# Page numbers read four at a time, and the experts' sub-keys moved to other slots, in a two-layer decoder step

## What is computed

```python
mla_past = cache_mla[i][page_table].reshape(B, past_len, KV_LORA + D_ROPE)
s = jnp.einsum('bqhc,bkc->bhqk', q_lat, ckv) + jnp.einsum('bqhr,bkr->bhqk', q_rope, krope)
p = jax.nn.softmax(s * MLA_SCALE, axis=-1)          # masked
return jnp.einsum('bhqk,bkc->bqhc', p, ckv)
```

```python
q = (tb @ wq).reshape(PEER_BLOCK, N_PEER_HEADS, 2, D_KEY_HALF)
s = jnp.einsum('thpk,hpnk->thpn', q, subkeys)
s_top, i_top = lax.top_k(s, TOPK)                   # 16 of 128, for each half of the key
cand = s_top[:, :, 0, :, None] + s_top[:, :, 1, None, :]
best, sel = lax.top_k(cand.reshape(..., 256), TOPK) # gives experts and the gates g
act = jax.nn.gelu(jnp.einsum('td,thkd->thk', tb, u[experts]), approximate=False)
return jnp.einsum('thk,thkd->td', g * act, v[experts])
```

## Time and profile before

| | us |
|---|---|
| median of three runs | 2816.77 |
| lowest and highest | 2816.19, 2819.77 |
| the profiled execution | 2811.99 |
| its span, first to last instruction | 2810.2 |

### The profile page before, as it was taken

How to read it: one execution, slowest core, us unless ns; L and a number is a source line. 1 busy time by engine, 2 the same in 40 slices (tenths; PEclk the granted TensorE clock), 3 DMA queues, 4 the chain that set the end, 5 groups by cost and what they waited for, 6 DMA issues and landing times. The chain is left out here.

```text
span 2810.2 us, 40500 instructions
## 1 busy us (share of the span) xinstructions
PE 2608.3 (93%) x16081; PEld 2165.7 (77%) x16081; DVE 1428.3 (51%) x3382; ACT 343.7 (12%) x1001; POOL 619.9 (22%) x619
## 2 busy tenths in 40 slices
PE   7879996699899999999999999898999999999997
PEld 5554473345479999999999957363999999999997
DVE  2320021020359987995555222212699699955553
ACT  2210020001211112110000010110211111100000
POOL 0004100000002333444333100000043244443330
PEclk9789997699999999999999999999999999999999
DMA  7778968997934998999999897669079899999995
GB/s 232 244 244 260 329 248 341 396 347 270 377 118 190 377 370 297 353 362 349 409 409 409 326 339 287 219 245 400 7 304 377 316 330 353 339 404 409 409 409 202
DMA packets 249098, 885.37 MB, mean 315 GB/s; under 512 B 27354, under 2 KB 34682, under 8 KB 238111
## 3 DMA queue, kind: packets, MB, share of 16 engines
q1 hardware_dynamic: 169342, 606.97, 58.2%
q0 software_dynamic: 79568, 275.81, 26.1%
HBM read 863.33 MB, written 109.08 MB: 346 GB/s over the span
## 5 line engine op out<-in xcount | busy, mean ns | idle before, releaser
L2788 PE MATMUL ps<-xT,front 128*128 128x192 f32 x4096 | 689.2, 327 | 9.6 <-issue 6.9
L2788 PEld LDWEIGHTS ps<-xT,front 128*128 128x128 f32 x4096 | 666.6, 191 | 14.1 <-issue 8.0
L2814 PE MATMUL ps<-p1e_S,p_qT 128*128 128x192 f32 x2048 | 337.1, 327 | 5.1 <-DMA p_qT<-in_peer_v 5.1
L2814 PE MATMUL ps<-p0e_S,p_qT 128*128 128x192 f32 x2048 | 337.0, 327 | 4.8 <-DMA p_qT<-in_peer_v 4.7
L2814 PEld LDWEIGHTS ps<-p1e_S,p_qT 128*128 128x128 f32 x2048 | 332.4, 190 | 9.6 <-DMA p_qT<-in_peer_v 9.6
L2814 PEld LDWEIGHTS ps<-p0e_S,p_qT 128*128 128x128 f32 x2048 | 332.4, 190 | 9.2 <-DMA p_qT<-in_peer_v 8.6
L2566 DVE CUSTOM_DVE_ANT_0 front<-front,x_tok 128x1024 f32<-128x1024 f32 x256 | 309.7, 1218 | 4.8 <-DMA front<-in_peer_u,p0e_expert 1.5
L2467 POOL DMA_INDIRECT front<-in_peer_u,p1e_expert x128 | 153.6, 1200 | 389.4 <-DVE p1e_dots L2566 207.4
L2467 POOL DMA_INDIRECT front<-in_peer_u,p0e_expert x128 | 153.5, 1199 | 388.8 <-DVE p0e_dots L2566 207.1
L2577 DVE SCALAR_TENSOR_TENSOR h_tok<-front,p0e_dots,h_tok 128x1024 f32<-128x1024 f32 x127 | 163.2, 1285 | 144.4 <-DMA front<-in_peer_v,p0e_expert 138.6
L2577 DVE SCALAR_TENSOR_TENSOR h_tok<-front,p1e_dots,h_tok 128x1024 f32<-128x1024 f32 x127 | 163.1, 1285 | 142.4 <-DMA front<-in_peer_v,p1e_expert 136.8
(11 more groups left out here) (464 smaller groups left out, 2930.9 us busy)
## 6 DMA issues: line engine op xcount, KB each, us to landing
front<-in_peer_uT SPq DMA_DIRECT2D x256, 512.0 KB
p_qT<-in_peer_v SPq DMA_DIRECT2D x256, 512.0 KB
out_swa_sample<-in_cache_swa_w SPq DMA_DIRECT2D x32, 2040.0 KB, 21.6
e_ring<-in_mla_pages SPq DMA_DIRECT2D x84, 272.0 KB, 3.8
e_ring<-in_swa_kT SPq DMA_DIRECT2D x16, 1024.0 KB, 9.2
e_arena<-in_swa_v SPq DMA_DIRECT2D x16, 1024.0 KB, 14.2
out_swa_sample<-in_cache_swa_w SPq DMA_DIRECT2D x8, 2016.0 KB, 31.5
e_ring<-in_attn_w_in SPq DMA_DIRECT2D x6, 2048.0 KB, 36.0
```

The costliest lines, as they stand in the source:

```text
L2788: mm = pe.matmul(k.ps[:, SB[i % len(SB)], 0:TD], ur[:, i % NU, c, :], k.xT[:, c, D0:T], start=(c == 0), stop=(c == KC - 1))
L2814: mm = pe.matmul(k.ps[:, c // 2, c % 2 * TD:(c % 2 + 1) * TD], vr[:, i % NV, c * P:(c + 1) * P], S[:, i, :], start=False, stop=(i == STEPS ...
```

## The change

There are three parts. First, `numbers` makes one load of four words instead of four loads, and still checks each number by itself. Second, SP reads the numbers of part n+9 right behind the transfers of part n, for every n from 7 to 22; nothing is read from part 23 on. Third, in the experts `subT` moves from the slots 2 and 3 of `ur` to the gather slots 4 to 6, and the candidates of the first tile from the gather slots 5 and 6 to 2 and 3. SP's wait for `scored` ahead of the blocks 2 and 3 goes, and POOL gets one ahead of gather 4. PE's wait for all twelve `s_ready` goes, and the steps 1, 2 and 3 wait for the copy of their own bank (`LAST_SCORE_IN`: 10, 11 and 12 copies); step 0 writes to bank 4 and waits for none.

```diff
     def numbers(self, sp, n):
         n_pool = self.k.io["mla_pages"].shape[0]
-        return [sp.value_load(self.table[0:1, 4 * n + j:4 * n + j + 1], min_val=0, max_val=n_pool - 1) for j in range(4)]
+        return self.k.nc.values_load_multi_w_load_instructions(
+            self.table[0:1, 4 * n:4 * n + 4], engines=[mybir.EngineType.SP], min_val=0, max_val=n_pool - 1)[1]
...
             for n in range(FIRST_PART, 4 * DEC_B):
-                numbers = latent.numbered[n] if n in latent.numbered else latent.numbers(sp, n)
                 wait(sp, v_used, n - PAGE_PARTS + 1)
-                latent.load_part(sp, slot(n), landed[n % PAGE_PARTS], numbers)
+                latent.load_part(sp, slot(n), landed[n % PAGE_PARTS], latent.numbered.pop(n))
+                if n + len(PARTS_NUMBERED_AHEAD) < 4 * DEC_B:
+                    latent.numbered[n + len(PARTS_NUMBERED_AHEAD)] = latent.numbers(sp, n + len(PARTS_NUMBERED_AHEAD))
                 if n % 4 == 3:
                     load_new(n // 4)
...
-        subT = uf[:, 2 * D:2 * D + TAIL].rearrange("p (a b) -> p a b", a=H2)
+        SUB_AT = 4 * D + D // 2
+        SUB_SLOTS = range(SUB_AT // D, (SUB_AT + TAIL - 1) // D + 1)
+        subT = gf[:, SUB_AT:SUB_AT + TAIL].rearrange("p (a b) -> p a b", a=H2)
...
-                 for x in (gf[:, 5 * D:7 * D], pf[:, 0:TAIL], pf[:, 0:TAIL])]
+                 for x in (gf[:, 2 * D:2 * D + TAIL], pf[:, 0:TAIL], pf[:, 0:TAIL])]
...
+        LAST_SCORE_IN = {QB + order % 3: order for order in range(len(SCORES))}
...
-                    if i in (2, 3):
-                        sp.wait_ge(scored, len(SCORES))
...
+                if n == SUB_SLOTS[0]:
+                    pool.wait_ge(scored, len(SCORES))
...
                 if i >= len(SB):
                     pe.wait_ge(gelu_done, i - len(SB) + 1)
+                elif SB[i] >= QB:
+                    pe.wait_ge(s_ready, LAST_SCORE_IN[SB[i]] + 1)
...
-            pe.wait_ge(s_ready, len(SCORES))
```

## The result

| | before | after |
|---|---|---|
| median, us | 2816.48 (4 runs) | 2788.11 (4 runs) |
| lowest and highest | 2814.80, 2819.77 | 2784.01, 2788.78 |
| profiled execution, its span | 2811.99, 2810.2 | 2788.78, 2787.0 |

The ratio is 0.9889, 95% interval 0.9877 to 0.9901. The medians differ by 28.4 us, and the ratio times the median of before gives 31.3 (27.9 to 34.6); 30.7 were forecast, and a time of 2786.1 against the 2788.1 measured.

A forecast was written before the change was run, and what follows sets the result against it. PE, busy 93% of the span, bounds the kernel; the end moves only where it idles or runs at half clock. Gains 2.8 + 18.2 + 9.7 = 30.7 take 2811.99 to 2781.3, plus 4.8 for the median: 2786.1; range 2777 to 2802.

The forecast's parts named there:

- The cost of a read: SP's read of a part's four page numbers: r = 1.35 us in place of 2.19, four checks of 0.25 kept.
- Rival 1: SP's load of four words takes four loads' time, r = 2.1: gain 21.3 us, time 2795.5; chance 0.17.
- Rival 3: Checks of SP's page numbers are cheap, partly waiting for the load, r = 0.86: gain 37.2, time 2779.6; chance 0.08.
- The barrier: Before the paged attention stage: SP reads numbers faster, so PE resumes at 101.2 in place of 103.97; gain 2.8 us.
- The pages: Paged attention: SP's reads set the pace of page transfers; with faster reads, 18.2 of 25.9 us lost are gained.
- what stays: Paged attention: 7.7 us of delay remain, holes of 2.1 and 2.4 at samples 4 and 5, each with 1.6 slow clock.
- The experts: Without PE's wait, step 0 follows the last score: 3.16 us of hole and 1.7 slow clock per layer, 9.7 in all.
- Rival 2: Experts: the last score really ends at 885.5, so only 0.65 of ACT's copy is gained: 22.3 in all, 2794.5; chance 0.16.
- the 7.8 us from step 0 to step 3: Experts: step 3 begins 7.8 us behind step 0, at 890.9, after the last copy it needs, done at 886.15.
- The 1.7 us of slow clock behind step 0: Experts: PE at clock 0.51 for 3.4 us in layer 0, costing 1.7; taken the same for layer 1, expected to go.
- The risks named for the experts' step: POOL's gathers 4 to 6 start 1.0 to 3.5 us later and DVE may slip; DVE's wait expected about 13.
- The slower rival: Paged attention: PE's clock stays at half in the denser stage; 5.9 us slower, 2822.7; chance 0.03.

The follow-up runs named there:

- unchecked: The whole change without the check that each loaded page number lies in the pool; ratio to the kernel before 0.9869.
- wait_all: The whole change, but PE waits for all twelve score copies ahead of step 0 of the experts again; ratio to the kernel before 0.9907.
- pool_waits: The kernel before with only the change's POOL wait for the last score ahead of gather 4 added; ratio to the kernel before 0.9972.
- pages_only: The first two parts of the change (four-word loads, reading nine parts ahead), with the experts as in the kernel before; ratio to it 0.9941.
- ahead_19: The whole change with numbers read twelve parts ahead in place of nine (parts 7 to 18 before the stage); ratio to the kernel before 0.9885.

## Why the prediction was right, point by point

**The cost of a read: right.** r = 1.35 was load 0.3 and four checks of 0.25. The load is 0.301 and the checks kept their 0.147; the nine reads in a row took 1.40 each. Rival 1 (four words cost four loads) is out, and with it, for SP's loads here, the Trainium skill's 200 ns for each register even in bulk (Runtime: NRT & Kernel Launch, Instruction fetch mechanics): three more words cost 35 ns. Rival 3 (the checks are mostly waiting for the load) is out too, as their duration didn't fall when the load was shared, and unchecked shows what leaving them out is worth.

**The barrier: right, the size with some luck.** The hole fell from 3.54 to 0.78, by 2.76; forecast 2.8. It is 0.78 in all eight kernels that read each part once with the batch. But with the reads of before it was 3.54, 2.60, 4.29 and 2.32 in the four traces, so the step is worth 1.5 to 3.5 us, and the trace from which the forecast was read lies in the middle.

**The pages: the mechanism right, the size some 4 us too large.** The stage from its first score to the projection behind it took 127.05 us and takes 112.46: 14.6 gained where the step said 18.2. The places were right in this trace (holes only at samples 4 and 5, though wait_all has one at 6), and so was the spacing of the parts, wide up to 23 and close behind it. The term that was mis-sized is what stays: 7.7 forecast, 11.5 measured (135.75 to 180.47, the scores 3 to 6, are 44.72 us, where three samples need 33.21). The holes are 3.11 and 2.85, 5.96 together where I wanted under 5, not 2.1 and 2.4, since the parts 16 to 19 took 16.3 us (136.06 to 152.37) in place of the 15.0 of 4 x 3.65 + 0.4. And the slow clock outlasts the score: sample 4 took 16.57 us from its score to the next (150.00 to 166.57), which is 2.65 more than 11.07 and the next hole, and sample 5 took 13.90, 2.83 more, where I had charged 1.6 each. The mean clock around sample 4 was 0.79:

```profile
146.90:162.90 16.00, 12.90 (x132) 8.93 (x133) 3.74 (x11) 2.26 (x5) 0.00 (x0) 0.79 0.88 282
```

By the ratios the pages with the barrier gave 16.6 (12.7 to 20.5), forecast 21.0.

**The experts: the number right, the reason only in part.** Step 0 follows the last score, and the lead grows by 3.24 at once in layer 0 (5.34 from the last scores to step 0 before, 2.10 after) and by 3.23 in layer 1; forecast 3.16. The slow clock went with it in both layers (1.00 from 864.8 to 874.0 and from 2035.3 to 2042.0). But the step said that PE's wait was the cause and held POOL's new wait for a risk alone. pool_waits and wait_all show the reverse: POOL's wait brings the hole from 3.16 to 0.68 by itself, PE's own wait is worth that 0.68. Rival 2 had seen rightly that the signal, not the row, was late, and was wrong in that the change left it so; what the removal of PE's wait alone would have given wasn't tried. (The row cited for the 7.8 us from step 0 to step 3 gives 8.7 for 48 of its matmuls; nothing hangs on it.) The 1.7 us of slow clock behind step 0, read in layer 0 and taken over for layer 1, hold there too in before (mean clock 0.76 from 2060.8 to 2068.0). But behind a hole of 3.19 in layer 0 of pages_only the clock stayed at 1.00, so it is not certain in every run. The risks named for the experts' step didn't come: DVE's wait for the exponentials is 11.6 us, forecast about 13.

```profile
DVE p0e_den L2559 <- ACT p0e_best L2706: 11.6, 1, 11.6
```

A part comes back later: in all steps PE now waits 4.6 us for the blocks of `peer_u`, where it waited 2.7 before. That fits with the lead, which between the last scores of layer 0 and those of layer 1 grows by 4.0 (18.1 to 22.2) and not by the 4.9 of hole and slow clock.

```profile
PE ps L2788 <- DMA front<-in_peer_uT: 2.7, 7, 0.8
...
L2795 PE MATMUL ps<-xT,front 128*128 128x192 f32 x4096 | 687.0, 327 | 4.7 <-DMA front<-in_peer_uT 4.6
```

**The slower rival (half clock in the denser stage): out.** The densest stage is that of unchecked, and from 117 to 198 it ran at the full clock (third number from the right):

```profile
117.00:198.00 81.00, 79.93 (x1019) 59.38 (x1015) 31.59 (x99) 18.35 (x36) 0.00 (x0) 1.00 0.84 302
```

**The sum.** 2.8 + 18.2 + 9.7 was 30.7. The runs give 16.6 for the first two terms together and 11.5 for the third, with some 4 us of uncertainty each; the pages were set too high and the experts, if anything, too low, so that the closeness of the total is in part luck. The base also helped: the 4.8 added for the distance of the profiled execution from the median were right, as the whole difference came out at 28.4 by medians though only at 23.2 by the two traces.

## What to carry to other kernels

An engine that only issues transfers has a pace too: count its instructions for each transfer, and where it is late, batch its reads of numbers and put what remains where it would wait anyway; spreading the reads gave, within the noise of the times, as much as leaving out their checks (the stage took 105.3 us against 101.4). Before removing a wait, ask whether the signal that it waits for is itself late and what runs beside it. Compare the ratios of several runs and not two traces where a few us matter, for single traces differed by 2 us at places that no edit touched.

## What the runs showed of the hardware

- A load of four words into SP's registers took 301 ns, of one word 266; each bounds check of a loaded number took 147 ns, and with all its gaps some 0.27 us ((1.40 - 0.30) / 4).
- Indirect gathers that POOL started beside and just behind the last matmuls of PE made a signal of PE's completion late: by 2.5 us with three gathers, in both layers of both kernels; by 1.2 us in one layer and 2.1 in the other with one (a single trace). Without them it came within 0.05 us in 21 of 22 cases, and once 0.7 late.
- Like idle times didn't always bring the half clock. Behind 1.42 us ahead of the cleared sums PE ran at full clock in one trace and at half in the other; in the paged attention the score's eight matmuls took 3.49 us behind a hole of 1.98 in before, and 1.94, the time at full clock, behind one of 2.72 in ahead_19.
- The stage of the paged attention, with the same reads, came out within 1.2 us from trace to trace, though its holes fell at different samples.
